# Attention scores as three products, results in the values' place, another order of the first tiles and of the row blocks

## The reference, cut to what matters

```python
u = h @ w_in                                # h = rmsnorm(x, norm_g)
c_q, c_kv, k_rope, z = jnp.split(u, ...)    # 384, 256, 32, 1024 columns
q = (rmsnorm(c_q, q_norm) @ w_q_b)          # 64 + 32 (rope) per head
kv = (rmsnorm(c_kv, kv_norm) @ w_kv_b)      # k 64, v 64 per head; k_rope is shared
for blk in range(S // Q_BLOCK):             # 8 row blocks of 128 queries
    q0, q1 = blk * Q_BLOCK, (blk + 1) * Q_BLOCK
    s = (q_nope[q0:q1] . k_nope[:q1] + q_rope[q0:q1] . k_rope[:q1]) * scale
    prob = softmax(where(k_chunk <= q_chunk, s, -inf))
    outs.append(prob @ v[:q1])
return (o * silu(z)) @ w_out
```

## Time and profile before

| | us |
|---|---|
| median of 3 runs | 2172.05 (2171.87 to 2172.08) |
| the profiled execution | 2172.23 |
| its span, first to last instruction | 2170.5 |
| TensorE busy | 1934.2 (89%) |
| VectorE, ScalarE, GpSimd busy | 814.6, 621.1, 511.1 |
| mean granted TensorE clock | 0.955 |

### The profile page before, as it was taken

How to read it: one execution, slowest core, us unless ns; L and a number is a source line. 1 busy time by engine, 2 the same in 40 slices (tenths; PEclk the granted TensorE clock), 3 DMA queues, 4 the chain that set the end, 5 groups by cost and what they waited for, 6 DMA issues and landing times. The chain is left out here.

```text
span 2170.5 us, 30302 instructions
## 1 busy us (share of the span) xinstructions
PE 1934.2 (89%) x11659; PEld 1327.1 (61%) x11659; DVE 814.6 (38%) x1457; ACT 621.1 (29%) x1325; POOL 511.1 (24%) x587
## 2 busy tenths in 40 slices
PE   6999999999899998999999889999969878888780
PEld 5998866666678776887887766666633223223220
DVE  5223345555433443442112347666531111111115
ACT  4333145555323433342122333232211111111111
POOL 2225231000021110001003576665211111111103
PEclk9999999999999999999999999999969999999895
DMA  5113371211221134641433422311569999999986
GB/s 194 50 40 120 136 220 26 50 25 45 107 83 44 46 68 100 91 74 61 115 111 103 161 79 74 103 55 55 228 247 390 425 425 423 424 419 419 420 351 243
DMA packets 101711, 371.75 MB, mean 171 GB/s; under 512 B 17413, under 2 KB 40138, under 8 KB 74698
## 3 DMA queue, kind: packets, MB, share of 16 engines
q1 hardware_dynamic: 83722, 323.59, 41.5%
q0 software_dynamic: 16704, 42.10, 5.0%
q10 hardware_dynamic: 1152, 4.19, 0.5%
HBM read 321.47 MB, written 65.14 MB: 178 GB/s over the span
## 5 line engine op out<-in xcount | busy, mean ns | idle before, releaser
L2806 PE MATMUL ps<-w_gu,rows_t 128*64 128x512 f32 x1024 | 262.5, 672 | 63.9 <-DMA w_gu<-w_up 62.2
L2806 PEld LDWEIGHTS ps<-w_gu,rows_t 128*64 128x64 f32 x1024 | 79.4, 153 | 224.0 <-issue 157.6
L930 PE MATMUL ps<-k_s,q_s 96*128 96x512 f32 (+3 forms) x384 | 150.7, 503 | 0.0
L2881 DVE TENSOR_TENSOR act_s<-act_g,ps 128x256 f32<-128x256 f32 x32 | 13.5, 421 | 334.2 <-ACT act_g L2872 334.2
L3064 POOL DMA_INDIRECT y_d<-y_out,asg_i x32 | 32.1, 1004 | 438.1 <-DVE y_out L2890 438.1
L2243 PE MATMUL ps<-w_o,mix_t 128*128 128x512 f32 x256 | 124.6, 615 | 0.0
L2824 PE MATMUL ps<-w_d,act_tt 128*64 128x512 f32 x512 | 116.9, 598 | 0.5 <-issue 0.5
L2872 ACT ACTIVATE act_g<-ps 128x256 f32<-128x256 f32 x32 | 12.3, 383 | 332.2 <-PE ps L2806 332.2
L484 PE MATMUL ps<-w_u_lo,x_hi 128*128 128x444 f32 (+2 forms) x256 | 93.8, 366 | 14.2 <-DVE x_lo L297 14.2
L1061 ACT ACTIVATE prob<-ps,stats 128x256 f32<-128x256 f32 (+7 forms) x128 | 94.6, 739 | 36.1 <-DVE stats L1024 35.1
L305 PE MATMUL ps<-tk_lo,h_hi 128*128 128x512 f32 x256 | 100.5, 392 | 3.0 <-DVE tk_lo L297 3.0
(11 more groups left out here) (457 smaller groups left out, 4056.3 us busy)
## 6 DMA issues: line engine op xcount, KB each, us to landing
w_gu<-w_gate SPq DMA_DIRECT2D x64, 1024.0 KB, 21.6
w_gu<-w_up SPq DMA_DIRECT2D x64, 1024.0 KB, 25.3
w_d<-w_down SPq DMA_DIRECT2D x64, 1024.0 KB, 19.1
w_tk<-w_in SPq DMA_DIRECT2D x5, 2048.0 KB, 13.0
proj_d<-tok_o POOLq DMA_DIRECT2D x40, 256.0 KB, 2.3
tk_in<-proj_d SPq DMA_DIRECT2D x8, 1280.0 KB, 6.1
yf<-y_d SPq DMA_DIRECT2D x4, 2048.0 KB, 14.2
w_ch<-w_in SPq DMA_DIRECT2D x12, 512.0 KB, 10.4
```

Source lines behind the costliest of these rows:

```text
L930: mm = pe.matmul(ps[:, b, 0:cn], q_s[p][:, a, i * P:(i + 1) * P], k_s[p][:, a, g * BANK:g * BANK + cn], start=True, stop=True)
L2806: mm = pe.matmul(ps[half, 2, :].rearrange("p (g n) -> p g n", g=2), rows_t[:, k, half], w_gu[q][:, h, :, k, :], start=(k == 0), stop=(k == ...
```

## The change

- The six small loads are issued by ScalarE; `positions` has a semaphore of its own, and the gain transposes wait only for the five others and come after x_turned(0). x_in[1] is loaded ahead of w_u[1].
- TensorE takes the first tiles in the order (0,0), (0,1), (1,0), (1,1), (0,2), (0,3), (1,2), (1,3). ScalarE and VectorE follow in a matching order; all of w_u[3]'s low part moves from GpSimd to VectorE, `angles` moves ahead of w_u_low(2).
- Scores are made of split products. GpSimd splits queries and keys of each pair (`split_heads`): two casts and two subtractions of 2 x 1024 columns, and once for each of the two buffers the rope rows of the keys. The low parts overwrite q_s and k_s. TensorE waits for the parts instead of for the loads. Pair 0 is loaded after query block 1, pair 1 (whose buffers lie where the latents were) only when A2's products are done. w_o is split in two halves around pair 2.
- o_ft lies in v_all's place: the results of pair u overwrite the values of pair u. Both copies of `outputs` come in slot 3 of the next pair.
- Row blocks of a pair are taken in the order 0, 7, 1, 6, 2, 5, 3, 4, with banks assigned to match.
- load_x(t) waits until o_t of tile t has been made, as res[t] lies over o_ft's tile t.

```diff
@@ -324,28 +324,27 @@
-            at_ = ROWS["norm_g"][0]
-            sp.dma_start(gain_rows[at_:at_ + 8, :], A["norm_g"].rearrange("a (k p) -> (a k) p", p=P)).then_inc(s_small, 16)
...
-            sp.dma_start(pos_i[:, :], A["positions"].rearrange("a (t p) -> p (a t)", p=P), allow_slow_non_contiguous=True).then_inc(s_small, 16)
...
+            sp.dma_start(x_in[1][:, :], A["x"][0, P:2 * P, :]).then_inc(s_xin[1], 16)
...
-                if g == 1:
-                    sp.dma_start(x_in[1][:, :], A["x"][0, P:2 * P, :]).then_inc(s_xin[1], 16)
...
+        def setup_act(act):
+            at_ = ROWS["norm_g"][0]
+            act.dma_start(gain_rows[at_:at_ + 8, :], A["norm_g"].rearrange("a (k p) -> (a k) p", p=P)).then_inc(s_small, 16)
...
+            act.dma_start(pos_i[:, :], A["positions"].rearrange("a (t p) -> p (a t)", p=P), allow_slow_non_contiguous=True).then_inc(s_pos, 16)
@@ -365,7 +364,7 @@
-            v.wait_ge(s_small, 6 * 16)
+            v.wait_ge(s_pos, 16)
@@ -443,15 +439,15 @@
-            for p in range(2):
-                for a in range(2):
-                    sp.dma_start(k_s[p][NOPE:QK, a, :], kr_d).then_inc(s_krin, 16)
+            load_k_rope(sp, 0)
...
-                if c == 2:
+                if c == 1:
...
-                if c == 3:
-                    load_heads(sp, 1)
...
+        def load_k_rope(sp, p):
+            for a in range(2):
+                sp.dma_start(k_s[p][NOPE:QK, a, :], kr_d).then_inc(s_krin[p], 16)
@@ -499,13 +492,25 @@
+            pe.wait_ge(s_const, 16)
...
-            for t in range(T - 2):
+            setup_pe(pe)
+            product(0, 0)
+            x_turned(1)
+            product(0, 1)
+            product(1, 0)
+            product(1, 1)
+            x_turned(2)
+            product(0, 2)
+            product(0, 3)
+            lat_turned(0)
+            product(1, 2)
+            product(1, 3)
+            for t in range(2, T - 2):
...
-                if t > 0:
-                    lat_turned(t - 1)
+                lat_turned(t - 1)
@@ -637,18 +651,31 @@
-            w_u_high(0)
+            w_u_high(0, (0,))
...
+            w_u_high(0, (1, 2, 3))
+            x_squared(1)
...
-            w_u_high(2)
+            x_high(1)
+            first_latents(0)
+            w_u_high(2, (0, 1))
+            last_latents(0)
+            w_u_high(2, (2, 3))
...
-            x_squared(1)
-            for t in range(T - 2):
+            latents(1)
+            normed(0)
+            silus(0)
+            x_squared(2)
+            x_high(2)
+            lat_high(0)
+            normed(1)
+            silus(1)
+            x_squared(3)
+            for t in range(2, T - 2):
...
-                if t > 0:
-                    lat_high(t - 1)
+                lat_high(t - 1)
@@ -743,18 +772,27 @@
-            w_u_low(0)
+            w_u_low(0, (0,))
...
+            w_u_low(0, (1, 2, 3))
+            x_gained(1)
...
+            x_low(1)
+            angles(v)
...
-            angles(v)
-            for t in range(T - 2):
+            w_u_low(3)
+            lat_squared(0)
+            lat_squared(1)
+            x_gained(2)
+            x_low(2)
+            lat_gained(0)
+            lat_low(0)
+            for t in range(2, T - 2):
...
-                if t > 0:
-                    lat_gained(t - 1)
-                    lat_low(t - 1)
+                lat_gained(t - 1)
+                lat_low(t - 1)
@@ -829,15 +867,20 @@
-            for i, ks in enumerate(w_u_pieces(3)):
-                wait(pool, s_wh, 12 + i + 1)
-                low(pool, w_u_lo[3][:, ks, :], w_u[3][:, ks, :], w_u_hi[3][:, ks, :]).then_inc(s_wl3, 1)
-            for t in range(T - 2):
+            x_rstd(1)
+            lat_rstd(0)
+            k_rotated(0)
+            lat_rstd(1)
+            k_rotated(1)
+            x_rstd(2)
+            z_stored(0)
+            k_stored(0)
+            z_stored(1)
+            for t in range(2, T - 2):
...
-                if t > 0:
-                    k_stored(t - 1)
+                k_stored(t - 1)
@@ -858,10 +901,13 @@
-        o_ft = sb("o_ft", [P, KD, S], o); o += 32 * KB
-        q_s = [sb(f"q_s{p}", [QK, 2, S], o + 8 * KB * p) for p in range(2)]; o += 16 * KB
-        k_s = [sb(f"k_s{p}", [QK, 2, S], o + 8 * KB * p) for p in range(2)]; o += 16 * KB
+        o_ft = sb("o_ft", [P, T, KD, P], at(0))
+        QK_AT = (136, 104)
+        q_s = [sb(f"q_s{p}", [QK, 2, S], at(QK_AT[p])) for p in range(2)]; q_lo = [sb(f"q_lo{p}", [QK, 2, S], at(QK_AT[p]), F32R) for p in range(2)]
+        q_hi = [sb(f"q_hi{p}", [QK, 2, S], at(QK_AT[p] + 8), F32R) for p in range(2)]
+        k_s = [sb(f"k_s{p}", [QK, 2, S], at(QK_AT[p] + 16)) for p in range(2)]; k_lo = [sb(f"k_lo{p}", [QK, 2, S], at(QK_AT[p] + 16), F32R) for p in range(2)]
@@ -875,17 +921,20 @@
-        SC = [[j % 4] if j < T else [2 * (j % 2), 2 * (j % 2) + 1] for j in range(NJ)]
-        PT = [[4 + j % 2] if j < T else [4, 5] for j in range(NJ)]
+        ROW = [0, 7, 1, 6, 2, 5, 3, 4]
+        row = lambda j: ROW[j // 2]
+        SC = [[0], [1], [2, 3], [0, 1], [2], [3], [0, 1], [2, 3]] * 2
+        PT = [[4 + j % 2] if row(j) < T // 2 else [4, 5] for j in range(NJ)]
...
-        o_jobs = Jobs(base, [6] * 4 + [7] * 4, PAIRS)
...
+        o_jobs = Jobs(base, [6 + i // 4 for i in ROW], PAIRS)
@@ -912,6 +961,8 @@
+            load_k_rope(sp, 1)
+            load_heads(sp, 1)
@@ -921,18 +972,18 @@
-                    mm = pe.matmul(ps[:, b, 0:cn], q_s[p][:, a, i * P:(i + 1) * P], k_s[p][:, a, g * BANK:g * BANK + cn],
...
+                    mm = split_products(pe, ps[:, b, 0:cn], [(q_hi[p][:, a, rows], q_lo[p][:, a, rows], k_hi[p][:, a, keys], k_lo[p][:, a, keys])])
@@ -966,9 +1018,7 @@
-                if u == 0:
-                    pe.wait_ge(s_krin, 64)
-                pe.wait_ge(s_pair[p], 48 * m + 48)
+                pe.wait_ge(s_qk, parts_made(u))
@@ -1002,8 +1052,10 @@
-            b = job_read(eng, o_jobs, 4 * half + 3, u)
-            dst = o_ft[:, bass.ds(u, 1), half * BANK:(half + 1) * BANK].rearrange("p a n -> p (a n)")
+            job_read(eng, o_jobs, T - 1, u)
+            b = job_read(eng, o_jobs, 6 + half, u)
+            dst = o_ft[:, 4 * half:4 * half + 4, bass.ds(u, 1), :].rearrange("p i a n -> p i (a n)")
+            b = b.rearrange("p (i n) -> p i n", i=4)
@@ -1059,26 +1111,26 @@
+                    outputs(act, u - 1 if j < NJ else u, 0)
...
-                    outputs(act, u, 0)
@@ -1086,11 +1138,39 @@
+            split_heads(pool, 1)
...
+                if k == 4:
+                    split_heads(pool, 2)
...
+            for u in range(3, PAIRS):
+                split_heads(pool, u)
...
+        def parts_made(u):
+            return ROTATED + 4 * u + 2 * min(u + 1, 2) + 4
...
+        def split_heads(pool, u):
...
+            p = u % 2
+            n = parts_made(u - 1) if u else ROTATED
+            if u < 2:
+                pool.wait_ge(s_krin[p], KR_IN[p])
+                pool.wait_ge(s_qk, n)
+                pool.tensor_copy(k_hi[p][NOPE:QK, :, :], k_s[p][NOPE:QK, :, :]).then_inc(s_qk, 1)
+                pool.wait_ge(s_qk, n + 1)
+                pool.tensor_tensor(k_lo[p][NOPE:QK, :, :], k_s[p][NOPE:QK, :, :], k_hi[p][NOPE:QK, :, :].bitcast(F32), ALU.subtract).then_inc(s_qk, 1)
+                n += 2
+                pool.wait_ge(s_qk, n)
+            pool.wait_ge(s_pair[p], 48 * (u // 2) + 48)
+            pool.tensor_copy(k_hi[p][0:NOPE, :, :], k_s[p][0:NOPE, :, :]).then_inc(s_qk, 1)
+            pool.tensor_copy(q_hi[p][:, :, :], q_s[p][:, :, :]).then_inc(s_qk, 1)
+            pool.wait_ge(s_qk, n + 1)
+            pool.tensor_tensor(k_lo[p][0:NOPE, :, :], k_s[p][0:NOPE, :, :], k_hi[p][0:NOPE, :, :].bitcast(F32), ALU.subtract).then_inc(s_qk, 1)
+            pool.wait_ge(s_qk, n + 2)
+            pool.tensor_tensor(q_lo[p][:, :, :], q_s[p][:, :, :], q_hi[p][:, :, :].bitcast(F32), ALU.subtract).then_inc(s_qk, 1)
@@ -1159,6 +1239,7 @@
+                wait(sp, bank_free[f_jobs.banks[1]], f_jobs.before(1, t) + 1)
@@ -3216,6 +3297,7 @@
+            split_heads(pool, 0)
```

More of the change, by code:

```diff
@@ L590, in x_high, with w_u_high, first_latents @@
                 high(act, x_hi[t % 2][:, :, :], x_t[t % 2][:, :, :]).then_inc(s_xhi, 1)
-            def w_u_high(g):
-                for i, ks in enumerate(w_u_pieces(g)):
+            def w_u_high(g, pieces=range(4)):
+                for i in pieces:
                     wait(act, s_win[4 if g == 0 and i >= 2 else g], 16)
+                    ks = slice(2 * i, 2 * i + 2)
                     high(act, w_u_hi[g][:, ks, :], w_u[g][:, ks, :]).then_inc(s_wh, 1)
-            def latents(t):
+            def first_latents(t):
                 p = t % 2
@@ L694, in x_low, with w_u_low @@
                 low(v, x_lo[t % 2][:, :, :], x_t[t % 2][:, :, :], x_hi[t % 2][:, :, :]).then_inc(s_xlo, 1)
-            def w_u_low(g):
-                for i, ks in enumerate(w_u_pieces(g)):
+            def w_u_low(g, pieces=range(4)):
```

(30 more changed lines are left out.)

55 lines of the change are left out of this document (28 added, 27 removed).

## The result

| | before | after |
|---|---|---|
| median of the runs, us | 2172.07 (2171.87 to 2174.45) | 2146.54 (2146.19 to 2147.45) |
| the profiled execution, us | 2172.23 | 2146.75 |
| its span, us | 2170.5 | 2144.9 |
| mean granted TensorE clock | 0.955 | 0.955 |

The ratio is 0.9878, with a 95% interval of 0.9866 to 0.9889: 25.5 us faster, where 30.2 were forecast (2142.0, range 2130 to 2160). I read the two traces against each other at six points, always at the same piece of work.

What follows compares the result with a forecast made beforehand. The prediction took TensorE to set the attention loop's pace (busy 277.2 of 289.7 us). Its terms for start, seven pairs, first pair and tail: 2172.2 - 10.5 - 18.9 + 0.5 - 1.3 = 2142.0 us, range 2130 to 2160.

Steps and rivals of the forecast that it cites:

- The start: Phase A's first tiles: first product at 13.0, a new 1.9 us wait, old hole gone, tile 1 done at 56.9; -10.5 us.
- Scores in three products: Attention loop: three fp32r products cost 0.68 against 0.86 at 512 columns; sixteen slots of a pair 14.1 us against 16.5.
- rival (a): Loop scores: narrow fp32r products at f32's price; 128 columns only 2152 (chance 0.10), 256 too +30 more, 2182 (0.04).
- the change-over of a slot: Score slots in the loop: 0.02 or 0.12 us added per slot, within the 14.1 us for sixteen slots.
- 34.2 of work and 1.8 of stalls: Loop of the kernel before: TensorE's work and stalls in us per pair, making up the measured period of 35.96.
- The row order: Loop: one 1.2 us stall at the second row 7, 1.3 of stalls per pair; period 33.3, 7 x -2.7 = -18.9.
- Rival (b): Loop: the latency chain binds in all big-row slots; stalls of 3 us a pair, period 35, 2155; chance 0.14.
- The first pair: Loop's first pair: no values to cover its row 7; 28.1 of work and 1.5 of stalls against 29.1, +0.5 us.
- GpSimd: Loop: splitting takes 13.3 us a pair, under a period of 33; pair 0 ready at 288, wanted at 289.0, zero cost.
- rival (c): Loop: GpSimd and VectorE shut each other out; two copies a pair held 3 us each, +48, 2190; chance 0.03.
- The tail: Loop's end to projection: product 3.1 earlier, but sz(2) behind a load waiting for o_t(1); -1.3 us kept (0 to -3).
- Rival (d): Start of the kernel: the new start does nothing because weights arrive no earlier; 2152, chance 0.05.

Runs made afterwards that it cites:

- start_only: The kernel after with the loop, layout and loads of before, so only the new start is left: 2163.38 us, ratio 0.9951.
- last_tile: The kernel after with x_turned(7) moved ahead of product(6,1), and x_high(7) and x_low(7) made one step earlier: 2143.23 us, ratio 0.9865.
- piece_first: The kernel after with two of the four w_u_low(1) pieces on VectorE before x_gained(1): 2144.52 us, ratio 0.9872.
- f32_scores: The kernel after with f32 scores straight from q_s and k_s and no splitting on GpSimd: 2163.06 us, ratio 0.9949.
- late_loads: The kernel after with pair 0 loaded one query block later, after block 2 instead of 1: 2150.67 us, ratio 0.9893.
- sz_first: The kernel after with SyncE issuing sz(2) between res(0) and w_g, ahead of the load waiting for o_t(1): 2141.13 us, ratio 0.9855.
- all_three: The kernel after with the edits of piece_first, last_tile and sz_first together: 2135.38 us, ratio 0.9826 against the kernel before.

## Why the prediction was right, and where it was off

**The start** was right to 0.2 us at its own end (first product 13.09 for 13.0, stall 1.99 for 1.9, tile 1 done 57.0 for 56.9). What failed is that the sum carries it to the end whole, with nothing put down for the rest of phase A: 1.5 us went to the clock behind the wait at x_lo(7). start_only shows the same loss, last_tile its end. That the kernel before escaped it is luck as far as the runs show: the wait was there before, and piece_first, with the new start, has full clock behind it.

**Scores in three products**: the direction and the narrow prices were right, so rival (a), narrow products at f32's price, is out. The mis-sized term is the change-over of a slot, "0.02 or 0.12", which I took from f32 slots. With fp32r products it is 0.04 to 0.13 in thirteen slots and 0.2 to 0.3 in three (387.19, 396.49 and 406.50, the first of them the slot with the stall): 2.1 us a pair where 1.1 had been charged. So scores were 15.1 a pair and not 14.1, 7 us over seven pairs. A second error is of the old kernel: I charged 34.2 of work and 1.8 of stalls to its period of 35.96, while its rows show one stall of 1.28 and the rest is work; f32_scores failed by the same term.

**The row order** behaved as reckoned: one stall a pair, at the forecast place, 0.80 and not 1.2, and none in slots 7 to 9. Of the forecast 0.5 less in stalls, 0.5 came. Rival (b), the latency chain in all big-row slots, would have shown several waits for prob_t a pair; the table has seven in the whole loop. The period is 33.8 for 33.3 (33.75 as the mean of seven): 1.0 more of scores, 0.1 more of transposes and 0.1 of values, 0.5 less of stall, and less 0.2 by which the forecast had rounded the work up; over seven pairs and against 35.96 that is 15.5 for 18.9. The first pair cost 0.8 for 0.5.

**GpSimd** hid all its work, and rival (c) is out: 684 ns a copy beside its casts and subtractions. The Trainium skill ("SBUF — State Buffer", Who interferes with whom) gives the exclusive lock against GpSimd to VectorE instructions with two SBUF inputs or in a two-port mode. The start fits its first half, 2.07 before and 0.29 after GpSimd's subtractions had left; the copies out of PSUM show no collision. For pair 0 "ready 288, wanted 289" became 278.5 and 279.8, a margin of 1.3 for 1.0, and late_loads prices its loss at about 4 us.

**The tail** gave 1.9 for 1.3. I named the new wait in SyncE's queue and called it covered by bytes that start 1.3 us earlier; in truth TensorE waits 4.34 and not 3.88 for the same load, and sz_first shows that 5.4 us by the medians were to be had there (clock included). The step that failed is to have weighed the queue only against before, not for what it holds back.

**Rival (d)**, no gain at the start, is out by start_only alone.

The terms close: of the 4.6 us by which the spans miss the forecast, 3.4 are the seven pairs, 1.5 the clock in phase A and 0.3 the first pair, less 0.6 of the tail. The layout (outputs in the values' place) had no run of its own; f32_scores has it together with the new row order, and its time equals that of start_only, so the two together neither gain nor cost while scores are f32.

## What to carry to other kernels

When an f32 product becomes three fp32r ones, count a tenth of a microsecond or a little more for each switch from other work, besides the products (here 2.1 us in 16 slots). A gain at the front of a program passes through every later wait: list these waits first, since each can take a part of it, in idle time and in the clock behind it. A removed wait gives its own length to the next stage; the clock behind it comes on top only if no other wait is followed by half clock in its stead. In a load queue, what waits for late work goes behind what the next stage needs.

## What the runs showed of the hardware

- fp32r products with 128 weight columns start 0.11 us apart at 128 moving columns, 0.12 at 256, 0.23 at 512. The Trainium skill ("TensorE: Matmul & The Clock Gate", LDWEIGHTS (loading the stationary operand)) has a weight load cost its columns over 1.2, 107 ns for 128. The spacing agrees, 0.11 and 0.12 up to 256 columns; the records of the weight loads themselves read 0.19 each and overlap, so they can't confirm it.
- The first fp32r product behind transposes or values takes 0.32 to 0.34 at 512 columns instead of 0.23. Four f32 products behind transposes take 1.72, 0.43 each with nothing added, and behind values 1.82. Why is open; no run took it apart.
- The same 2.77 us wait was followed by full clock in two profiled kernels (before, piece_first) and by half clock, worth 1.7 us, in the six others that have it. The 2.24 us wait before the projection did the same: half clock in seven of the ten kernels (0.57 to 0.67 over the four us behind it), 1.00 in last_tile, sz_first and all_three. The stretches of work that lead to the waits are alike; what decides was not found.
- Casts and subtractions of GpSimd go by columns, not by partitions: 1.89 for 2048 columns on 32, 64 or 96 partitions, and 4.5 to 4.6 for the subtraction.
